# Modulation vectors of a two-part transformer: matrix-vector products on TensorE, or on VectorE with a sum over partitions

## The reference

```python
s_lat = jax.nn.silu(c)          # one vector of 1024
s_ctx = jax.nn.silu(c_ctx)      # another one
...                             # for each layer i of 2
mod = (s_lat @ w_mod[i] + b_mod[i])[:, None, :]     # w_mod[i]: 1024 x 6144
mod_c = s_ctx @ w_mod[i] + b_mod[i]
sh1, sc1, g1, sh2, sc2, g2 = jnp.split(mod, 6, axis=-1)
```

## Time and profile before

| | |
|---|---|
| median of three runs | 3853.12 us |
| span of the profiled execution | 3848.4 us |
| TensorE busy | 3718.6 us, 97% |
| VectorE busy | 2396.7 us, 62% |
| ScalarE busy | 1577.5 us, 41% |
| GpSimd busy | 840.9 us, 22% |

### The profile page before, as it was taken

The page is one execution under the profiler, slowest core; times in us unless marked ns, Lnnn a source line. Parts: engine busy times, 40 slices in busy tenths (PEclk is TensorE's granted clock), DMA queues, the critical chain, the costliest instruction groups (busy, mean ns, idle before and its releaser), DMA issues.

```text
span 3848.4 us, 56344 instructions
## 1 busy us (share of the span) xinstructions
PE 3718.6 (97%) x22665; PEld 3215.4 (84%) x22665; DVE 2396.7 (62%) x4154; ACT 1577.5 (41%) x2538; POOL 840.9 (22%) x695
## 2 busy tenths in 40 slices
PE   8999999989999999999999999998999999899998
PEld 5788777788899899999999999777777777677887
DVE  6455433466899668888888887567533345764333
ACT  4523343444335653333333335446422243653222
POOL 0112000153116454344344343010100010100000
PEclk9999999999999999999999999999999999899999
DMA  5211245533355679999999995320333432112332
GB/s 206 82 47 45 91 141 184 194 108 100 96 175 190 221 253 358 345 330 346 325 345 332 346 333 184 94 76 28 111 121 126 137 131 69 58 39 88 99 95 75
DMA packets 213908, 647.03 MB, mean 168 GB/s; under 512 B 19760, under 2 KB 65840, under 8 KB 210064
## 3 DMA queue, kind: packets, MB, share of 16 engines
q1 hardware_dynamic: 162816, 459.47, 35.8%
q0 software_dynamic: 50832, 183.95, 13.1%
HBM read 615.13 MB, written 27.79 MB: 167 GB/s over the span
## 4 chain that ended last, share of the span: by engine, by line
PE 86%; DVE 8%; ACT 4%; issue 1%; DMA 1%; POOL 0%; SPq 0%; DVEq 0%; ACTq 0%
PE ps L600 22%; PE ps L611 22%; PE ps L602 21%; PE ps L557 4%; PE ps L3502 2%; PE ps L2544 1%; PE ps L2571 1%; PE ps L2562 1%; PE ps L909 1%; DVE hlo_plain L774 1%; ACT l_NS L2594 1%; PE ps L2147 1%; PE ps L1240 1%; PE ps L1575 1%; PE ps L1231 1%
## 5 line engine op out<-in xcount | busy, mean ns | idle before, releaser
L600 PE MATMUL ps<-hhi,whi 128*128 128x512 f32 (+1 forms) x2824 | 1060.5, 376 | 3.6 <-DVE xres L3089 2.9
L532 DVE TENSOR_TENSOR wlo<-raw,whi 128x1024 fp32r<-128x1024 f32 x543 | 666.6, 1228 | 598.7 <-ACT whi L524 588.9
L602 PE MATMUL ps<-hlo,whi 128*128 128x512 f32 (+1 forms) x2824 | 1033.1, 366 | 0.2
L524 ACT ACTIVATE whi<-raw 128x1024 fp32r<-128x1024 f32 x616 | 648.5, 1054 | 596.9 <-PE ps L611 410.2
L611 PE MATMUL ps<-hhi,wlo 128*128 128x512 f32 (+1 forms) x2824 | 653.7, 370 | 0.0
L600 PEld LDWEIGHTS ps<-hhi,whi 128*128 128x128 f32 x2824 | 532.7, 189 | 104.1 <-issue 23.5
L602 PEld LDWEIGHTS ps<-hlo,whi 128*128 128x128 f32 x2824 | 531.7, 188 | 68.8 <-issue 4.1
L611 PEld LDWEIGHTS ps<-hhi,wlo 128*128 128x128 f32 x2824 | 499.8, 188 | 73.8 <-issue 6.8
L600 PE MATMUL ps<-ag_hi,whi 128*128 128x352 f32 x1024 | 328.6, 324 | 0.0
L602 PE MATMUL ps<-ag_lo,whi 128*128 128x352 f32 x1024 | 327.6, 321 | 0.0
L532 POOL TENSOR_TENSOR wlo<-raw,whi 128x1024 fp32r<-128x1024 f32 x74 | 183.8, 2492 | 161.0 <-ACT whi L524 158.8
(11 more groups left out here) (677 smaller groups left out, 6208.5 us busy)
## 6 DMA issues: line engine op xcount, KB each, us to landing
raw<-w_in SPq DMA_DIRECT2D x151, 512.0 KB, 3.8
raw<-peer_u SPq DMA_DIRECT2D x128, 512.0 KB, 6.6
raw<-peer_v SPq DMA_DIRECT2D x128, 512.0 KB, 6.2
raw<-w_mod SPq DMA_DIRECT2D x96, 512.0 KB, 4.1
raw<-w_gate SPq DMA_DIRECT2D x66, 512.0 KB, 3.6
raw<-w_up SPq DMA_DIRECT2D x66, 512.0 KB, 3.6
raw<-w_down SPq DMA_DIRECT2D x66, 512.0 KB, 3.6
gate_dram<-stage SPq DMA_DIRECT2D x22, 1024.0 KB, 4.7
```

What stands on the lines that cost most here:

```text
L524: a.x.activation(whi[n % NW][:], raw[i % NRAW][:], ACT.Copy, bias=0.0, scale=1.0).then_inc(*a.gives("hi", i))
L532: e.x.tensor_tensor(wlo[n % NW][:], raw[i % NRAW][:], whi[n % NW][:].bitcast(F32), ALU.subtract).then_inc(*e.gives(*lo_sig(i)))
L600: t.x.matmul(o, w, p.hi, start=grp.opens and k == 0, stop=False)
L602: t.x.matmul(o, w, p.lo, start=False, stop=False)
```

## The change

The products move from TensorE to VectorE. For each modulation slab `mod_vector` multiplies the 128 x 1024 floats by one column of `svec`, partition by partition, and adds them to an accumulator `macc` in SBUF. It does so once for each of the two vectors, so there are two instructions per slab. In thirds 1 and 2 of layer 1 only the vector of the 512 tokens is used, and one instruction is left. After eight slabs (a half of a third) `mod_sum` lets TensorE add up the 128 partitions with a column of ones out of `sel`. That takes two matmuls for each accumulator, 32 columns of weights and 512 moving columns.

The key of a slab is now (layer, third, half, chunk): the eight chunks of a half follow each other, and the next half reuses the accumulator, so its first product waits for the sum of the half before. A raw buffer is free when VectorE has done its last product. `between` replaces `coupled`: slabs stand singly, one or two after a unit, not as pairs. The last third of layer 1 now stands wholly inside the feed-forward layer.

```diff
+def between(main, other):
+    out, n = [], 0
     for i, u in enumerate(main):
-        upto = -(-blocks * (i + 1) // len(main))
-        out += halves[2 * n:2 * upto] + [u]
+        upto = min(len(other) * (i + 1) // (len(main) - 1), len(other))
+        out += [u] + other[n:upto]
...
-            y.wait_ge(*(("mod_t", i - NRAW) if before.kind == "mod" else end(i - NRAW) if before.direct else lo_sig(i - NRAW)))
+            y.wait_ge(*(mod_done(i - NRAW) if before.kind == "mod" else end(i - NRAW) if before.direct else lo_sig(i - NRAW)))
...
-    def mod_tensor(t, i):
-        l, r, k, half = spine[i].key
-        if k == 0 and half == 0:
-            hold(t, mod_at[l, r], ("mod_v", l, r, 0), ("mod_v", l, r, 1))
-        t.wait_ge(f"raw{i % NRAW}", i)
-        t.wait_ge("svec_a")
-        for j in (2 * half, 2 * half + 1):
-            ins = t.x.matmul(bank[mod_at[l, r]][32 * j:32 * j + 32, :], svec[:, 2 * k:2 * k + 32],
-                             raw[i % NRAW][:, 512 * (j % 2):512 * (j % 2) + 512], start=k == 0, stop=k == KC - 1,
-                             tile_position=(0, 32 * j))
-        ins.then_inc(*t.gives("mod_t", i))
+    def mod_vector(v, i):
+        l, r, half, k = spine[i].key
+        v.wait_ge(f"raw{i % NRAW}", i)
+        v.wait_ge("svec_a")
+        if k == 0:
+            for f in [("modsum_t", l, r, 0)] if half else mod_free.get((l, r), []):
+                v.wait_ge(*f)
+        for w in mod_vectors(l, r):
+            acc, col = mod_acc[l, r][w], svec[:, 2 * k + w:2 * k + w + 1]
+            if k == 0:
+                ins = v.x.tensor_scalar(acc[:], raw[i % NRAW][:], col, None, ALU.mult)
+            else:
+                v.wait_ge("modacc_v", l, r, half, k - 1, w)
+                ins = v.x.scalar_tensor_tensor(acc[:], raw[i % NRAW][:], col, acc[:], ALU.mult, ALU.add)
+            ins.then_inc(*v.gives("modacc_v", l, r, half, k, w))
...
+        def tensor(t):
+            yield Ready(("modacc_v", l, r, half, KC - 1, n - 1), ("sel_g", 1), *(freed.get(mod_at[l, r], ()) if half == 0 else ()))
...
+            for w in range(n):
+                for x in range(2):
+                    j = 2 * half + x
+                    ins = t.x.matmul(b[32 * j:32 * j + 32, :], sel[:, 1 - w:33 - w], mod_acc[l, r][w][:, 512 * x:512 * x + 512],
+                                     start=w == 0, stop=w == n - 1, tile_position=(0, 32 * j))
...
-    spine += u_dn[:2] + coupled(u_dn[2:], m0[:16]) + u_da[:-12] + coupled(u_da[-12:], m0[16:32]) + u_merge[:4] + u_z
-    spine += coupled(u_merge[4:] + u_out[:6], m0[32:] + m1[:16]) + u_out[6:]
+    spine += u_dn[:2] + between(u_dn[2:], m0[:16]) + u_da[:-12] + between(u_da[-12:], m0[16:32]) + u_merge[:4] + u_z
+    spine += between(u_merge[4:] + u_out[:6], m0[32:] + m1[:16]) + u_out[6:]
...
-    spine += lm0.units + u_lout[0] + net0.units[:2] + m1[16:18] + coupled(net0.units[2:], m1[18:44])
-    spine += lm1.units[:2] + m1[44:] + lm1.units[2:] + u_lout[1] + net1.units
+    spine += lm0.units + u_lout[0] + net0.units[:2] + between(net0.units[2:], m1[16:])
+    spine += lm1.units + u_lout[1] + net1.units
```

More of the change, by code:

```diff
@@ L847, in first_gpsimd @@
         g.x.memset(ones[:], 1.0).then_inc(*g.gives("ones_g"))
-        g.x.memset(svec[:], 0.0).then_inc(*g.gives("svec_g"))
+        g.x.memset(sel[:], 0.0).then_inc(*g.gives("sel_g", 0))
+        g.wait_ge("sel_g", 0)
+        g.x.memset(sel[:, 1:2], 1.0).then_inc(*g.gives("sel_g", 1))
     def first_scalar(a):
@@ L894, in svec_scalar @@
                        ACT.Silu, bias=0.0, scale=1.0).then_inc(*a.gives("svec_a"))
[L898 removed]
+    msb = [sb(f"msb{i}", kb, [512]) for i, kb in enumerate((DA + 34, WK + 70, WK + 94, 134, 158, 171))]
     mod_at = {(0, 0): 6, (0, 1): 5, (0, 2): 6, (1, 0): 7, (1, 1): 6, (1, 2): 7}
[L900 to L912 removed]
+    mod_acc = {lr: [sb(f"macc{lr[0]}{lr[1]}{w}", kb + 4 * w, [1024]) for w in range(2)]
+               for lr, kb in (((0, 0), 113), ((0, 1), 97), ((0, 2), 155), ((1, 0), 155), ((1, 1), 161), ((1, 2), 161))}
@@ new lines, in program, with mod_vectors @@
+    mod_free = {(0, 2): [("z_v", "lo", 3)], (1, 0): [("modsum_t", 0, 2, 1)], (1, 2): [("modsum_t", 1, 1, 1)]}
+    def mod_vectors(l, r):
+        return range(1 if l == 1 and r else 2)
+    def mod_vector(v, i):
[13 more added lines that the diff above has]
+            ins.then_inc(*v.gives("modacc_v", l, r, half, k, w))
@@ new lines, in mod_done, with mod_sum @@
+    def mod_done(i):
+        l, r, half, k = spine[i].key
+        return ("modacc_v", l, r, half, k, mod_vectors(l, r)[-1])
+    def mod_sum(l, r, half):
+        b, n = bank[mod_at[l, r]], len(mod_vectors(l, r))
+        def tensor(t):
+            yield Ready(("modacc_v", l, r, half, KC - 1, n - 1), ("sel_g", 1), *(freed.get(mod_at[l, r], ()) if half == 0 else ()))
+            if half == 0:
+                hold(t, mod_at[l, r], ("mod_v", l, r, 0), ("mod_v", l, r, 1))
+            t.wait_ge("sel_g", 1)
+            t.wait_ge("modacc_v", l, r, half, KC - 1, n - 1)
+            for w in range(n):
[3 more added lines that the diff above has]
+                                     start=w == 0, stop=w == n - 1, tile_position=(0, 32 * j))
+            ins.then_inc(*t.gives("modsum_t", l, r, half))
+        return {"tensor": tensor}
@@ L914, in mod_end @@
     def mod_end(l, r, free):
-        last = place_of["mod", (l, r, KC - 1, 1)]
         b, m = bank[mod_at[l, r]], msb[3 * l + r]
         def scalar(a):
-            a.wait_ge("mod_t", last)
+            a.wait_ge("modsum_t", l, r, 1)
             for f in free:
@@ L926, in tensor @@
         def tensor(t):
+            yield from mod_sum(l, r, 1)["tensor"](t)
             yield 0.3
@@ L955, in mod_ready @@
         return ("mod_v", l, 2, "gain", 1)
-    mods = [[Unit("mod", (l, r, k, h), io["w_mod"][((3 * l + r) * 8 + k) * 2 + h], T, [], None)
-             for r in range(3) for k in range(KC) for h in range(2)] for l in range(2)]
+    mods = [[Unit("mod", (l, r, h, k), io["w_mod"][((3 * l + r) * 2 + h) * 8 + k], T, [], None)
+             for r in range(3) for h in range(2) for k in range(KC)] for l in range(2)]
     evac = {}
@@ L1418, in vector @@
                     begun.add(n)
+                    v.wait_ge("modsum_t", 0, 0, 1)
                     v.x.tensor_copy(oacc[:, n], heads(bank_of(step, "out"))).then_inc(*v.gives(cw, "out", step))
@@ L1676, in z_scalar @@
             a.wait_ge("z_v", "gated", h)
+            a.wait_ge("modsum_t", 0, 1, 1)
             a.x.activation(odn_hi[:, h], zs[:, h], ACT.Copy, bias=0.0, scale=1.0).then_inc(*a.gives("z_a", "hi", h))
@@ L3948, in perform @@
         elif kind == "mod":
-            if e.name == "tensor":
-                mod_tensor(e, what)
+            if e.name == "vector":
+                mod_vector(e, what)
     plan = Weave(perform, {e: Clocked(Tally(nc), e, Blank(e)) for e in ENGINES})
@@ L4011, in mod_piece @@
         raw_done(i)
-        l, r, k, half = spine[i].key
-        if k == KC - 1 and half == 1:
+        l, r, half, k = spine[i].key
+        if k == KC - 1 and half == 0:
+            plan.start(f"modsum{l}{r}", mod_sum(l, r, 0))
+        elif k == KC - 1:
             free = {(0, 1): [("chain0_v", "out", 3), ("chain1_v", "out", 3)], (0, 2): [("da_v", "oda", 3, 3)], (1, 0): [last_of("merge", KC - 1)]}.get((l, r), [])
```

9 lines of the change are left out of this document (2 added, 7 removed).

## The result

The changed kernel takes 3912.64 us (median of 4 runs, 3910.5 to 3913.81), beside 3852.77 of the kernel before (4 runs). The ratio is 1.0156, 95% interval 1.0143 to 1.0168: 60 us slower. The forecast was 3878 us with 3846 to 3902 as its range. The direction was right, the size was not, and the time lies outside the range.

The account below looks back on a forecast made before the run. TensorE, busy 97% of the span, was taken as the bound, with VectorE becoming it in the first stretch. Stretches of +28, 0, +7 and -15 us plus +5 for the clock gave +25 on 3853: 3878 us, range 3846 to 3902.

Parts of the forecast that it names:

- the term for the clock: First stretch: five idle times of about 6 us lower TensorE's clock, 0 to 8.5 us, taken as +5.
- TensorE's relief and the sums: All four stretches: 48 slab pairs at 1.22 us leave TensorE, -58.6 us; twelve added sums cost 21.7 us.
- The first stretch: Earliest stretch with modulation slabs, units 4 to 12 in a loop: VectorE becomes the bound, +28 us before the clock.
- Loads add 0.8 us twice: First stretch: a buffer freed by a product is needed two VectorE instructions later, 0.8 us at two places.
- The loop through VectorE: Units 4 to 12: four products delay the remainder the next unit needs, turns of 11.4 us against 5.44 or 6.66; +28 us.
- rival B: Only VectorE's total work counts, not the loop: +11.5 us in the first stretch, -6 overall, 3847 us; chance 0.15.
- The second stretch: Units 36 to 50: TensorE gains 5.6 us, attention steps wait 0 to 12 us for VectorE, taken together as 0.
- The third stretch: Units 57 to 85: TensorE gains 11.1 us, late remainders at eight places cost 14 to 22 us, taken as +7.
- The fourth stretch: Thirds 1 and 2 of the second layer: pairs removed -19.5 us, sums +4.9, remainders in time, so -15 us.
- rival D: Outside the first stretch the slabs were hidden anyway, so removing their 48.8 us brings nothing: 3927 us; chance 0.02.
- Rival A: TensorE's relief counts in full because VectorE's work overlaps: -37 us, 3816 us; chance 0.07.
- Rival C: Late products delay attention steps: second and third stretches +12 and +15, lower clock there +5, 3903 us; chance 0.09.

Follow-up runs that it names:

- free_and_small: Changed kernel with products reading constants, so slab buffers are free at landing, and 140 of 160 products on 64 columns: 3819.22 us, 0.9904 of the kernel before.
- raw_free_early: Changed kernel with products reading constants times zero instead of the slab, so its buffer is free at landing: 3845.12 us, 0.9974 of the kernel before.
- warm_first: Changed kernel with eight more matmuls before each first-stretch unit that follows a slab, filling TensorE's wait: 3927.24 us, 1.0176 of the kernel before.

## Why the prediction was too low, point by point

Two steps failed. The forecast's path was wrong: it let TensorE wait for the remainder `wlo`, and most of the waiting is for `whi` (50.4 us, beside 12.1), behind loads whose buffer a product had held. And the term for the clock was mis-sized: +5 us forecast, 33 measured. Of the 37 us that the sum of the stretches is off (+62 against +25), 28 are the clock; the rest is -3 in the first stretch, +7 in the third and +5 in the fourth.

- **TensorE's relief and the sums: right.** Without waits the first three stretches are 5.6, 7.5 and 11.6 us shorter than before (free_and_small); forecast were 5.6, 5.6 and 11.1. (In the second, 1.5 us of it are idle time of the kernel before.) A small sum was taken as 1.2 us. In the trace of the changed kernel the matmul start before it is at 3005.13, the sum at 3005.45 and the second start behind it at 3006.77, which is 1.64 us where two steps of 0.23 would stand: 1.2.

```profile
3005.13 0.39 PE L601 MATMUL ps<-hlo,whi 128*128 128x512 f32 x1
3005.45 1.05 PE L941 MATMUL ps<-macc,sel 128*32 128x512 f32 x4
3006.43 0.50 PE L599 MATMUL ps<-hhi,whi 128*128 128x512 f32 x1
3006.77 0.39 PE L601 MATMUL ps<-hlo,whi 128*128 128x512 f32 x1
```

- **The products: right.** A median of 1280 ns and about 750 for the first of eight, VectorE at 2577.7 us; forecast near 2580.
- **The first stretch: the right direction by the wrong mechanism.** The step that failed is "Loads add 0.8 us twice". The walk let TensorE wait only in front of the last matmuls, for the remainder, and took it that a late load costs a unit little. In fact the wait stands in front of the first matmul, and the whole unit of 5.44 us comes after it. TensorE waits 22.5 us for `whi` and 7.7 for `wlo`:

```profile
PE ps L599 <- ACT whi L523: 22.5, 6, 5.4
PE ps L610 <- DVE wlo L531: 7.7, 2, 3.9
```

 The profile's signs had been TensorE idle some 25 us between 50 and 130 us behind `wlo`, and VectorE over 90% busy there. It is idle 22 us, but mostly behind `whi`, and VectorE is 75% busy (60.29 of 80 us): it waits in the loop too. That +37.6 stands so near +33 is partly luck. The loop through VectorE, sized at 28 net, measures 11.3 with the buffers free (raw_free_early), where VectorE hardly waits; that is rival B's rule for this stretch. As the remainders had moved forward there as well, what the loop would cost in the forecast's own order stays open.
- **The clock: right sign, mis-sized, and the largest part of the miss.** +5 us and the first stretch alone; measured 13.0 there, 5.9 in the second and 14.0 in the third. The earlier trace rows had the price, but it was applied to the first stretch alone. The second had been given no idle time on balance, and the third's 14 to 22 us of late remainders no clock.
- **The second stretch: 0 forecast, +6.1 measured**, of which 5.9 are the clock. The 7.7 us of idle time are not steps of the attention, as forecast, but nearly all late `whi`:

```profile
PE ps L599 <- ACT whi L523: 7.0, 3, 2.5
```

- **The third stretch: +7 forecast, +28.1 measured**, the largest miss. The forecast did name "loads whose buffer a product frees" and priced them inside "remainders come 1 to 5 us late at eight places, 14 to 22 us". Measured are 25.8 us of idle time, of which

```profile
PE ps L599 <- ACT whi L523: 20.9, 7, 4.5
PE ps L610 <- DVE wlo L531: 4.4, 1, 4.4
```

 and on top the 14.0 us of clock that the sum didn't have. So of the 21 us missed, some 7 to 8 are idle time that was sized too small and 14 are the clock, which the sum didn't have here.
- **The fourth stretch: -15 forecast, -9.6 measured.** The working missed that four of the sixteen pairs were free already. They stand just outside the table's fourth stretch, which holds the other twelve (96 records). In the kernel before, two pairs stand where TensorE waits for `hhi` of a new norm, at 3121.34, and two more at 2738.26:

```profile
2738.26 1.92 PE L909 MATMUL ps<-raw,svec 128*32 128x512 f32 x16
2742.59 0.47 PE L630 MATMUL ps<-hhi,whi 128*128 128x512 f32 x1 [2.41 <-ACT hhi L741]
...
3121.34 1.92 PE L909 MATMUL ps<-raw,svec 128*32 128x512 f32 x16
3125.68 0.47 PE L630 MATMUL ps<-hhi,whi 128*128 128x512 f32 x1 [2.41 <-ACT hhi L741]
```

 In the changed kernel the pairs are gone and the wait is longer by as much:

```profile
2815.79 0.77 PE L629 MATMUL ps<-hhi,whi 128*128 128x512 f32 x1 [4.26 <-ACT hhi L740]
...
3190.16 0.77 PE L629 MATMUL ps<-hhi,whi 128*128 128x512 f32 x1 [4.26 <-ACT hhi L740]
```

 So twelve pairs count: 12 x 1.22 = 14.6, less four sums of 1.2, is -9.8. This is rival D in a small place. The fourth window of the earlier trace rows began behind the first of these places, and the wait at the second is nearly all of its idle 1.7 us, which I passed over.
- **Rival A** (-37 us) is what free_and_small measures, -38. Its sum was right; its condition, that VectorE's work lies beside TensorE's and holds nothing, is not met. The rule of the Trainium skill cited there (Perfetto Trace Analysis, Identifying the Most-Contended Engine) is to optimize the most contended engine first, and the forecast read from it that taking work off TensorE is a gain. Here that held in the fourth stretch (-9.6 us) and not in the first three together (+72).
- **Rival C** (3903 us) came nearest to the time, and not by its mechanism: it priced attention steps in the second and third stretches at +12 and +15 and the clock at 5 more. Measured are +6.1 and +28.1, and the waits are for `whi`.

## What to carry to other kernels

When work moves to another engine, ask first what it holds while it waits for its turn there. In a ring of four buffers, consumers that stand in a slower or waiting engine's order set when the next loads start, and a late load stops TensorE in front of a whole unit. Writing the same 160 instructions earlier in the order took back 53 of 60 us here. Then price each idle time twice, once for the wait and once for the clock after it. And before removing work counts as a gain, look in order of time at whether it already fills a wait; a busy share of a window doesn't show that.

## What the runs showed of the hardware that I had not expected

- The slower clock adds half as much again to the idle time that causes it: 33 us on top of 64 us in the first three stretches of the changed kernel. Single waits there are at most 5.4 us long, and the mean granted clock is 0.88, 0.96 and 0.92.
- In warm_first 20.4 us more of busy TensorE in 129 us (107.66 against 87.23) left the granted clock at 0.89. The idle times were shorter there and more of them (18.4 us in six, 3.2 in four).
- A VectorE product of 128 x 1024 from a landed slab keeps its 1280 ns while transfers of 140 to 175 GB/s run beside it (the stretches' last column): of 140 in the changed kernel the median is 1280 and the mean 1304 ns, and four are longer than 1.3 us, the longest 2.31. Together those four add some 3 us of VectorE's time, so a slowdown by contention is not what cost the 60.
